# Seven block products of eight for the unit pairs of the last feed-forward layer

## The reference

```python
D_MODEL = 1024; D_FF = 4 * D_MODEL

def squared_relu_mlp(h, w1, w2):
    return jnp.square(jax.nn.relu(h @ w1)) @ w2

def trunk(x, ...):
    for l in range(DEPTH):          # DEPTH = 2
        ...                         # mixer of layer l, x = x + rmsnorm(mix, gl[1])
        h = rmsnorm(x, gl[2])
        x = x + rmsnorm(squared_relu_mlp(h, w_ff1[l], w_ff2[l]), gl[3])
```

## Time and profile before

| | us |
|---|---|
| median of 3 runs | 2652.76 |
| lowest, highest | 2652.28, 2657.85 |
| the profiled execution: its own time | 2653.71 |
| the profiled execution: its span | 2651.5 |

### The profile page before, as it was taken

The page is one execution under the profiler, slowest core; times in us unless marked ns, Lnnn a source line. Parts: engine busy times, 40 slices in busy tenths (PEclk is TensorE's granted clock), DMA queues, the critical chain, the costliest instruction groups (busy, mean ns, idle before and its releaser), DMA issues.

```text
span 2651.5 us, 39319 instructions
## 1 busy us (share of the span) xinstructions
PE 2586.9 (98%) x16324; PEld 2309.3 (87%) x16324; DVE 1381.3 (52%) x2201; ACT 1127.9 (43%) x1914; POOL 244.4 (9%) x396
## 2 busy tenths in 40 slices
PE   8998989899999999999999999999999999999998
PEld 7778888788787798899999989998877888999998
DVE  4746765656564475534444465535544456444344
ACT  6654446455444245333333345433332344333324
POOL 4121111100001001100000001110000000000000
PEclk9999999999999999999999999999999999999999
DMA  6453344432333445543333245554434343233322
GB/s 204 157 158 104 106 117 135 148 102 85 106 88 98 119 143 161 174 123 111 105 93 109 87 128 153 165 147 125 119 120 147 100 118 125 85 110 109 96 88 82
DMA packets 368721, 321.47 MB, mean 121 GB/s; under 512 B 11929, under 2 KB 339667, under 8 KB 368544
## 3 DMA queue, kind: packets, MB, share of 16 engines
q1 hardware_dynamic: 336224, 207.91, 27.1%
q0 software_dynamic: 32320, 111.05, 13.7%
HBM read 261.33 MB, written 57.58 MB: 120 GB/s over the span
## 4 chain that ended last, share of the span: by engine, by line
PE 84%; DVE 7%; ACT 5%; DMA 2%; issue 2%; SPq 0%; DVEq 0%; ACTq 0%
PE dense L591 74%; PE mixer L591 8%; DVE wlo L1651 1%; ACT arena L1134 1%; ACT whi L1134 1%; DVE arena L1876 1%; DMA wst<-in_w_ff_dram 1%; DVE arena L1878 1%; DMA arena<-xrow 0%; ACT relu L1134 0%; DVE hf L1792 0%; DMA wst<-in_w_in_even_dram 0%; DMA xrow<-arena 0%; ACT L1134 0%; ACT h1hi L1134 0%
## 5 line engine op out<-in xcount | busy, mean ns | idle before, releaser
L591 PE MATMUL dense<-hhi,whi 128*128 128x272 f32 (+1 forms) x3072 | 848.7, 331 | 20.7 <-DVE wlo L1651 15.1
L591 PE MATMUL dense<-hhi,wlo 128*128 128x272 f32 (+1 forms) x3072 | 825.5, 323 | 0.0
L591 PE MATMUL dense<-hlo,whi 128*128 128x272 f32 (+1 forms) x3072 | 825.4, 323 | 0.0
L1651 DVE TENSOR_TENSOR wlo<-wst,whi 128x1024 fp32r<-128x1024 f32 x384 | 471.3, 1227 | 231.6 <-ACT whi L1134 230.7
L1134 ACT ACTIVATE whi<-wst 128x1024 fp32r<-128x1024 f32 x384 | 403.8, 1052 | 424.9 <-PE dense L591 414.4
L591 PEld LDWEIGHTS dense<-hhi,whi 128*128 128x128 f32 x3072 | 516.5, 189 | 77.0 <-DVE wlo L1651 20.8
L591 PEld LDWEIGHTS dense<-hhi,wlo 128*128 128x128 f32 x3072 | 515.2, 189 | 41.9
L591 PEld LDWEIGHTS dense<-hlo,whi 128*128 128x128 f32 x3072 | 517.1, 189 | 37.3 <-issue 0.7
L591 PE MATMUL dense<-h1hi,whi 128*128 128x272 f32 (+1 forms) x1536 | 422.7, 329 | 12.6 <-DVE wlo L1651 8.1
L591 PE MATMUL dense<-h1hi,wlo 128*128 128x272 f32 (+1 forms) x1536 | 413.8, 324 | 0.0
L591 PE MATMUL dense<-h1lo,whi 128*128 128x272 f32 (+1 forms) x1536 | 412.1, 322 | 0.0
(11 more groups left out here) (352 smaller groups left out, 1815.6 us busy)
## 6 DMA issues: line engine op xcount, KB each, us to landing
wst<-in_w_ff_dram SPq DMA_DIRECT2D x256, 512.0 KB, 4.0
wst<-in_w_in_even_dram SPq DMA_DIRECT2D x48, 512.0 KB, 4.1
wst<-in_w_in_odd_dram SPq DMA_DIRECT2D x48, 512.0 KB, 4.0
proj<-ffh POOLq DMA_DIRECT2D x48, 272.0 KB, 2.6
proj<-ffh POOLq DMA_DIRECT2D x48, 256.0 KB, 2.3
arena<-proj POOLq DMA_DIRECT2D x16, 512.0 KB, 4.8
wst<-in_w_out_even_dram SPq DMA_DIRECT2D x16, 512.0 KB, 4.2
arena<-proj POOLq DMA_DIRECT2D x8, 1024.0 KB, 8.0
```

Of the source, the lines that this page charges most:

```text
L591: return pe.matmul(out, lhsT, rhs, start=start, stop=stop)
L1651: TT(wlo[:, u % 2, :], wst[:, u % 2, :], whi[:, u % 2, :].bitcast(F32), ALU.subtract)\
```

## The change

Blocks f = 2..7 of the last MLP layer of group 1 (l = 1, g = 1) change, and with them the side work before.

- **Products.** The two f1 units of a pair (k = 0, 1 or 2, 3) and the 544 tokens are taken as 2 by 2 by 2 blocks: two output blocks of 128, two halves of the 1024 inputs (`KH` = 4 steps of 128), two token halves (`XC` = 272). Seven block products with sums of weights and sums of inputs replace the eight. A product n = 0..6 ("p" item) is 4 steps of 3 matmuls of 272 columns. A pair is 84 matmuls, where two units were 96. f2 units stay.
- **Weight splits.** `hi` and `lo` now run per product on 512 columns (`split_part`), in a ring of five quarters (two halves each of `whi` and `wlo`'s two buffers, the fifth in the idle `hhi[0]`/`hlo[0]`), three products ahead. `hi(r)` waits until the product after the quarter's last user has begun.
- **Weight sums.** GpSimd makes the sums of weights of each pair (`weight_sums`, four additions of 128x512; the third writes into the raw weights).
- **Input sums.** VectorE makes four sums of inputs and splits them once (`x_sums`, items "t" 0..4, on 128x1088), in blocks f = 1.
- **Results.** Products 0 and 2 are copied out by VectorE, 3 by ScalarE (`keep`, in `accA`); 1, 4 and 5 are added to them by VectorE into `relu2`; 6 goes through relu on ScalarE. Relu and both squares run per token half on ScalarE. Bank by bank, product 2 adds to what 0 left in PSUM, 4 to 2, 6 to 4, and 5 to 3, so each waits until the earlier one is read (`SEVEN_AFTER`).
- **Side work.** Normalisation and output tiles of group 0 stand in the first 34 pieces of the layer, where they were spread over 240; the "t" items follow in 18 pieces. Raw weights of the second pair (k = 2, 3) go to `accA`.
- **Everywhere.** The first f2 unit of every block walks its eight steps in another order (`steps_of`). Three semaphores for constants become one.

The plan:

```diff
+SEVEN_READ = ("dve", "dve", "dve", "act", "dve", "dve", "act")
+SEVEN_BANK = "XYXZXZX"
+SEVEN_AFTER = {2: 0, 4: 2, 5: 3, 6: 4}
+XC = GN[1] // 2
+KH = KT // 2
...
-        return [(0, 0), (0, 1), (0, 2), (1, 0), (1, 1), (1, 2), (0, 3), (1, 3)]
+        return [(0, 0), (0, 1), (1, 0), (1, 1), (0, 2), (1, 2), (0, 3), (1, 3)]
...
+                self.ahead["d", u, 0] = [r + 1] if r + 1 < len(self.ops) else []
+                if u + 1 in self.pair:
+                    self.ahead["d", u, 2] = [r + 2]
+            elif u in self.pair:
+                r = self.op[u, 0]
+                for n in range(7):
+                    self.ahead["p", u, n] = [r + n + 3]
+                if k == 0:
+                    self.ahead["p", u, 0] = [r + 2, r + 3]
+                else:
+                    self.ahead["p", u, 4], self.ahead["p", u, 5], self.ahead["p", u, 6] = [], [r + 7], []
...
-        self.mix(rows[:-16], rest(2) + self.norm(14, False) + [("y", t) for t in range(4)] + rest(12))
+        n = 2 * PIECES[1] * FK * SEVEN[0]
+        self.mix(rows[:n - 30], rest(2) + self.norm(14, False) + [("y", t) for t in range(4)])
+        self.mix(rows[n - 30:n - 12], [("t", 0), ("t", 1), ("t", 2), ("t", 3), ("t", 4), ("rest",)])
+        self.mix(rows[n - 12:-16], [])
```

SyncE (weight loads) and TensorE:

```diff
+                before = PLAN.before_raw[u]
+                if before is not None:
+                    sp.wait_ge(S("w_split"), PLAN.last_op(before) + 1)
+                elif u >= 2:
+                    sp.wait_ge(S("t_split"), 4)
+                if u >= 2 and before != u - 2:
+                    sp.wait_ge(S("w_hi"), PLAN.first_op(u - 2) + 1)
...
+            def seventh(u, n):
+
+                r = PLAN.op[u, n]
+                pe.wait_ge(S("w_split"), r + 1)
+                if PLAN.pair[u] == 0 and n in (2, 3, 4, 6):
+                    pe.wait_ge(S("t_split"), {2: 2, 3: 1, 4: 4, 6: 3}[n])
+                fresh = n not in SEVEN_AFTER
+                if fresh:
+                    begin((u, n))
+                else:
+                    evac_wait(pe, (u, SEVEN_AFTER[n]))
...
+                for t in range(KH):
+                    for i, (w, x) in enumerate(((wh, xh), (wh, xlow), (wl, xh))):
```

ScalarE:

```diff
+            def hi(r):
+                u, n = PLAN.ops[r]
+                if PLAN.free[r]:
+                    act.wait_ge(S("w_used"), PLAN.free[r])
...
+                if n in (0, 1, 6):
+                    v = u + n // 6
+                    act.wait_ge(S(f"w_loaded{v % 2}"), 16 * (v // 2 + 1))
+                else:
+                    act.wait_ge(S("w_sum"), 3 * PLAN.pair[u] + {2: 1, 4: 1, 3: 2, 5: 3}[n])
+                A_(split_part(whi, hhi[0], PLAN.quarter[r]), raw_part(u, n), ACT.Copy).then_inc(S("w_hi"), 1)
...
+            def seventh(u, n):
+
+                f = PLAN.ff1_rank[u]
+                done((u, n))
+                out = DB[:, PLAN.jobs[u, n]["bank"], 0:XC]
+                if n == 3:
+                    if PLAN.pair[u]:
+                        evac_wait(act, (min(v for v in PLAN.pair if PLAN.pair[v] == PLAN.pair[u] - 1), 4))
+                    A_(keep[:, 1, :], out, ACT.Copy).then_inc(S("act_evac"), 1)
...
+            def summed(u, n):
+
+                v, c0 = u + (n == 4), XC * (n > 1)
+                r = relu2[:, PLAN.ff1_rank[v] % 2, c0:c0 + XC]
+                evac_wait(act, (u, n))
+                after(own(A_(r, r, ACT.Relu)))
+                last = squares(v, c0, c0 + XC)
+                if n == 5:
+                    last.then_inc(S("h1_hi"), 1)
...
+                if item[0] == "p":
+                    if item[2] in (3, 6):
+                        seventh(*item[1:])
+                    elif item[2] == 2:
+                        summed(item[1], 1)
+                    elif item[2] == 5:
+                        summed(item[1], 4)
+                        summed(item[1], 5)
```

VectorE:

```diff
+            def x_sums(i):
...
+                    link(TT(tsum, h12, h11, ALU.subtract))
+                    link(TT(tsum, tsum, l12, ALU.add))
+                    link(TT(tsum, tsum, l11, ALU.subtract))
...
+                    done((min(PLAN.pair) - FK - 1, 0))
+                    link(TT(tsum, h22, h12, ALU.subtract))
+                    link(TT(tsum, tsum, l22, ALU.add))
+                    link(TT(tsum, tsum, l12, ALU.subtract))
+                n = {1: 3, 2: 2, 3: 6, 4: 4}[i]
+                link(dve.tensor_copy(t_part(hhi, n), tsum))
+                TT(t_part(hlo, n), tsum, t_part(hhi, n).bitcast(F32), ALU.subtract).then_inc(S("t_split"), 1)
...
+            def seventh(u, n):
+
+                f = PLAN.ff1_rank[u]
+                if PLAN.units[u][4] and n in (1, 3):
+                    h1_rest(u - 2 + n // 3)
+                if SEVEN_READ[n] != "dve":
+                    return
+                out = DB[:, PLAN.jobs[u, n]["bank"], 0:XC]
+                if n in (1, 4, 5):
+                    evac_wait(dve, (u, {1: 0, 4: 3, 5: 2}[n]))
+                if n in (1, 4):
+                    dve.wait_ge(S("h1_split"), f - 1 + n // 4)
+                done((u, n))
+                if n in (0, 2):
+                    dve.tensor_copy(keep[:, n, :], out).then_inc(S("dve_evac"), 1)
+                    return
+                r = relu2[:, (f + (n == 4)) % 2, XC * (n > 1):XC * (n > 1) + XC]
+                TT(r, out, keep[:, {1: 0, 4: 1, 5: 2}[n], :], ALU.add).then_inc(S("dve_evac"), 1)
...
+                if kind == "f2" and k == 0 and PLAN.seven("f1", l, g, a):
+                    h1_rest(u - 2)
...
+                elif item[0] == "p":
+                    if item[2] == 0:
+                        seventh(*item[1:])
+                    for r in PLAN.ahead[item]:
+                        lo(r)
+                    if item[2]:
+                        seventh(*item[1:])
```

GpSimd:

```diff
+            def weight_sums(u):
...
+                step(add(sums[:, 0, :], a11, a21, ALU.subtract))
+                add(sums[:, 1, :], a22, sums[:, 0, :], ALU.subtract).then_inc(S("w_sum"), 1)
+                add(a21, a21, a22, ALU.add).then_inc(S("w_sum"), 1)
+                pool.wait_ge(S("w_split"), PLAN.op[u, 1] + 1)
+                pool.wait_ge(S("w_sum"), 3 * p + 1)
+                add(a12, a12, sums[:, 1, :], ALU.subtract).then_inc(S("w_sum"), 1)
```

More of the change, by code:

```diff
@@ L112, in ff @@
             for k in range(FK):
-                rows += self.unit("f1", l, g, f, k)
+                if not self.seven("f1", l, g, f):
+                    rows += self.unit("f1", l, g, f, k)
+                elif k % 2 == 0:
+                    u = len(self.units)
+                    self.units += [("f1", l, g, f, k), ("f1", l, g, f, k + 1)]
+                    rows += [[("p", u, n)] for n in range(7)]
             for k in range(FK):
@@ L643, in piece @@
                         last.then_inc(S("job_done"), 1)
+            def seventh(u, n):
[9 more added lines that the diff above has]
+                out = DB[:, PLAN.jobs[u, n]["bank"], 0:XC]
+                wh, wl = split_part(whi, hhi[0], PLAN.quarter[r]), split_part(wlo, hlo[0], PLAN.quarter[r])
+                xh, xlow = x_part(hhi, n), x_part(hlo, n)
+                for t in range(KH):
+                    for i, (w, x) in enumerate(((wh, xh), (wh, xlow), (wl, xh))):
+                        last = pe.matmul(out, w[:, t * P:(t + 1) * P], x[:, t, :], start=fresh and t == 0 and i == 0,
+                                         stop=t == KH - 1 and i == 2, skip_group_check=True)
+                        if t == 0 and i == 0:
+                            last.then_inc(S("w_used"), 1)
+                last.then_inc(S("job_done"), 1)
             def x_in(t):
@@ L1588, in _ @@
                     hi(0)
-                if item[0] == "d":
-                    if item[2] == 0:
-                        hi(item[1] + 1)
+                for r in PLAN.ahead.get(item, ()):
+                    hi(r)
+                if item[0] == "p":
[6 more added lines that the diff above has]
+                        summed(item[1], 5)
+                elif item[0] == "d":
                     for key in PLAN.ends[item]:
@@ L2254, in _ @@
                         unit_begin(item[1])
-                    if item[2] == (1 if item[1] else 2):
-                        lo(item[1] + 1)
+                    for r in PLAN.ahead.get(("d", item[1], item[2] - 1 - (item[1] == 0)), ()):
+                        lo(r)
                     if item[1] in PLAN.after_conv:
```

166 lines of the change are left out of this document (144 added, 22 removed).

## The result

The changed kernel takes 2659.52 us (median of 21 runs, 2653.43 to 2661.52), the kernel before 2655.25 in the same sessions (21 runs, 2652.28 to 2657.85): a ratio of 1.0017, 95% interval 1.0011 to 1.0023. That is 4.3 us more, 2.9 to 6.1 by the interval. The prediction had +7.7, against the 2652.76 of the first three runs.

The account below looks back on a forecast made before the run. TensorE was taken as the bound, busy 98% of the span. -18.0 + 7.2 + 2.5 + 0.4 + 15.6 = +7.7 on 2653.71 us gave 2661.4, as a median 2660.5; 8-in-10 range 2645 to 2672.

Parts of the forecast that it names:

- within: Outcome class: a difference from the kernel before of no more than about 0.2%, 5.3 us; chance 0.22.
- The gain: Two pairs in six blocks, each 84 matmuls instead of 96, at 0.125 us a matmul: -18.0 us.
- The pauses: Input sums on VectorE before block 2 make TensorE stand 2.1 us, then 5.1 more than before: 7.2 us together.
- Clock: TensorE at half pace after the two input-sum pauses: 2.5 us for both, between 1.7 and 3.4.
- the case shown: Earlier trace: after a late split, 2.51 us between TensorE's matmuls, then half pace, 1.7 us lost.
- Packed side work: Eight group 0 steps stand 3.4 us apart on average instead of 13: 0.4 us, range 0 to 2.
- The blocks: Waits in the six blocks of seven products, 2.6 us a block: 15.6 us, from 4.2 to 38.
- product 6 starts 1.1 to 1.8 late: First pair of a block: splits 6 and 0 and add 4 end late beside GpSimd's sums, delaying product 6.
- The hold: GpSimd's additions make VectorE instructions with two SBUF inputs stand, even earlier starters; without it 0.7 us a block.
- Rival 1: In the blocks, begun splits finish and GpSimd's additions slip at no cost: -4.5, 2648.3 us; chance 0.20.
- Rival 2: The ring of weight splits hides all in the blocks, input sums cost their pauses alone: -10.8, 2642 us; chance 0.13.
- Rival 3: ScalarE saturates in the pairs, the second never catches up, half pace in every block: +27, 2680 us; chance 0.17.

Follow-up runs that it names:

- experiment 1: Changed kernel with each of the 18 input-sum operations cut to 4 of 272 columns (wrong results): 2647.20 us, ratio 0.9971 to the kernel before.
- experiment 4: Changed kernel with the 18 input-sum operations placed one by one, at most one behind a piece, all work kept: 2649.46 us, ratio 0.9976.
- experiment 2: Changed kernel with GpSimd's four additions of a pair cut to 16 of 512 columns (wrong results): 2653.47 us, ratio 0.9995.
- experiment 3: Changed kernel with VectorE copying product 2 out of PSUM early in each block's second pair: 2659.15 us, ratio 1.0014.
- experiment 5: As experiment 3, and ScalarE also copies product 3 early in the second pair: 2652.34 us, ratio 0.9994.
- experiment 7: Changed kernel with spread input sums, both second-pair copies early and a new step order in f2's first unit: 2638.40 us, ratio 0.9940.

## Why the prediction was right, and which terms were not

The side was right (slower), and the change 3.4 us too large (7.7 where 4.3 was measured). By the prediction's own bar, that a difference can be told from 5.3 us on, 4.3 still counts as "within", to which it gave 0.22; with 21 runs of each kernel the interval, 2.9 to 6.1, doesn't reach down to 0. By its steps:

- **The gain, -18.0.** Right: 144 matmuls fewer, and between stops the pace is 0.125.
- **The pauses, 7.2.** Right in place, cause and size: between starts 2.18 and 5.54, less the 0.32 that stood there before, is 7.4. Experiments 1 and 4 show the cause.
- **Clock, 2.5 of 1.7 to 3.4.** The changed kernel's trace shows 1.6, those of experiments 2, 3 and 5 show 4.2. The error was to take the pause of 2 us as below the case shown; half pace followed it in three of these four traces. The upper bound was too low.
- **Packed side work, 0.4.** The one stop that grew before the first pause (TensorE at 2274.69 after a wait of 0.52, where it had 0.21 before) costs 0.3 more.
- **The blocks, 15.6.** The mis-sized term: 6 x 1.95 = 11.7. The copy was late as worked out (1.07, of 0.9 to 1.05 predicted), the relu in f2 0.39 where 0.25 was said. What failed is the step "product 6 starts 1.1 to 1.8 late": it is 0.30. I had let the split stand through all three of GpSimd's additions, from 5.1 to 8.9. They take turns instead, a split waits for the rest of one, and GpSimd's additions grow from 1.3 to 1.62 and 1.74. The longest split is 1.82, where over 3 was to show the forecast right. The hold is real: experiment 2 gives it 0.96 us a block (0.99 more than before without it, 0.7 predicted), where the forecast had 1.9.

Together: -18.0 + 7.4 + 1.6 + 0.3 + 11.7 = +3.0 by the trace, against 3.5 between the two traces (0.5 stays unexplained), and +5.6 with the clock as in experiment 3. The measured 4.3 lies between. Part of the closeness is luck: the blocks were put 3.9 too high, and the clock 1.7 too low wherever half pace follows both pauses.

**Rival 1** said that the hold costs nothing. Half of its mechanism is what happens: a split that runs is finished and GpSimd slips. But a split that comes second waits, and that is not free. Of the Trainium skill's rule (SBUF — State Buffer, Who interferes with whom: the one that issues first keeps the shared ports for its whole instruction, the other is blocked) I had written that the trace disagrees, by the earlier trace rows. The turns of this trace agree with it throughout, even where VectorE came first by only 0.09 us, in experiment 7:

```profile
2528.90 1.74 POOL L2917 TENSOR_TENSOR wst<-wst 128x512 f32<-128x512 f32 x1
```

```profile
2528.81 0.68 DVE L1860 TENSOR_TENSOR wlo<-wst,whi 128x512 fp32r<-128x512 f32 x1
```

What I hadn't looked at in the earlier trace rows is what GpSimd did just ahead of its addition. Both times it was issuing a DMA, and VectorE's instruction (336.88 and 477.65) began within that; the first of the two issues:

```profile
336.30 0.68 POOL L2514 DMA_DIRECT2D arena<-arow  x1 [2.34 <-DMA arow<-arena]
```

A DMA issue alone doesn't hold a split: at 42.51 one that starts within such an issue, with a one-input 32x32 instruction of GpSimd behind it, takes its usual time.

```profile
42.51 1.23 DVE L1651 TENSOR_TENSOR wlo<-wst,whi 128x1024 fp32r<-128x1024 f32 x1 [1.13 <-ACT whi L1134]
```

Why an addition behind a DMA issue goes ahead of a split that began up to 0.31 us earlier wasn't tried and stays open. There the order of starts does not decide. It doesn't bear on the sum, since no DMA issue stands ahead of the weight sums.

**Rival 2** (faster, 2642) had the input sums right and the blocks wrong. **Rival 3** (saturation) didn't come: a block loses 2.34 us, not 4, and the granted clock in the blocks is 1.00.

## What to carry to other kernels

Saving TensorE work moves the bound to the order of the helper queues. Here the 18 us that fewer matmuls saved were paid back by two lumps of VectorE work ahead of a split, and by copies queued behind work that nobody was waiting for. The same work in another order is 21 us faster. Cut work that is needed once into pieces, and put them behind, not ahead of, what TensorE waits for next. When a wait goes and the time stays, look one product further, on the other engine's queue, before giving up the idea.

## What was not expected of the hardware

- VectorE with two SBUF inputs and GpSimd alternate instruction by instruction: 0.69 becomes up to 1.82 on the one side, 1.29 becomes 1.62 to 1.83 on the other. An addition of VectorE with one input in PSUM is untouched (0.43).
- A stop of TensorE costs more than the wait that the profile shows: 0.16 us shown are 0.32 to 0.39 between starts, and 0.84 are 1.07.
- The same pause of 2.0 us was followed by half pace in three executions of the same code and not in a fourth, and one of 5.4 us cost 1.6 or 2.7 us beyond itself.
